# Gate and up products of a SwiGLU block: one 512-column product for the rounded weight against both activation halves, alternating with a 256-column product for the weight's low half

## What is computed

```
D_MODEL = 1024; SEQ = 256; DEPTH = 2; D_FF = 2816

def swiglu(x, wg, wu, wd):
    return (jax.nn.silu(x @ wg) * (x @ wu)) @ wd

for l in range(DEPTH):
    x = layer_norm(ALPHA * x + 0.5 * swiglu(x, ffn1_wg[l], ffn1_wu[l], ffn1_wd[l]), ln1_g[l], ln1_b[l])
    ...
    x = layer_norm(ALPHA * x + 0.5 * swiglu(x, ffn2_wg[l], ffn2_wu[l], ffn2_wd[l]), ln4_g[l], ln4_b[l])
```

## Time and profile before

| | us |
|---|---|
| three runs | 1675.73, 1677.74, 1677.77 |
| median | 1677.74 |
| the profiled execution | 1675.35 |
| its span, first to last instruction | 1673.5 |
| PE / PEld / DVE / ACT / POOL busy | 1616.8 / 1495.3 / 1109.6 / 757.1 / 291.8 |
| granted TensorE clock, mean | 0.993 |

### The profile page before, as it was taken

The page is one execution under the profiler, slowest core; times in us unless marked ns, Lnnn a source line. Parts: engine busy times, 40 slices in busy tenths (PEclk is TensorE's granted clock), DMA queues, the critical chain, the costliest instruction groups (busy, mean ns, idle before and its releaser), DMA issues.

```text
span 1673.5 us, 33031 instructions
## 1 busy us (share of the span) xinstructions
PE 1616.8 (97%) x14330; PEld 1495.3 (89%) x14330; DVE 1109.6 (66%) x1409; ACT 757.1 (45%) x977; POOL 291.8 (17%) x190
## 2 busy tenths in 40 slices
PE   8999999999999998999999999999999999999996
PEld 7899989989889987999889898899898989889995
DVE  4676599868456758444576756998674658574445
ACT  3554453652253544444455445346433535454442
POOL 1133420000000305101150434100000004040102
PEclk9999999999999999999999999999999999999998
DMA  7766644433446545666676566544334455456663
GB/s 200 223 183 176 201 139 141 128 121 107 125 114 193 174 137 146 186 187 185 203 184 183 175 181 184 152 142 130 96 116 128 131 197 166 141 157 181 187 188 115
DMA packets 380777, 267.84 MB, mean 160 GB/s; under 512 B 21117, under 2 KB 361561, under 8 KB 380633
## 3 DMA queue, kind: packets, MB, share of 16 engines
q1 hardware_dynamic: 377784, 255.25, 52.2%
q10 hardware_dynamic: 2848, 10.49, 1.7%
HBM read 264.66 MB, written 1.05 MB: 159 GB/s over the span
## 4 chain that ended last, share of the span: by engine, by line
PE 79%; DVE 15%; ACT 3%; issue 2%; DMA 1%; POOL 0%; SPq 0%; DVEq 0%; ACTq 0%; POOLq 0%
PE bank L714 15%; PE bank L715 14%; PE bank L716 14%; PE bank L727 7%; PE banks4to L716 6%; PE banks4to L715 6%; PE banks4to L714 6%; DVE ring_lo L1696 4%; PE bank L756 1%; DVE small L1715 1%; DVE x_tok L1710 1%; ACT ring_hi L1306 1%; PE banks4to L1096 1%; PE bank L1261 1%; PE bank L1245 1%
## 5 line engine op out<-in xcount | busy, mean ns | idle before, releaser
L1696 DVE TENSOR_TENSOR ring_lo<-ring_raw,ring_hi 128x1024 fp32r<-128x1024 f32 x438 | 585.3, 1342 | 373.2 <-ACT ring_hi L1306 369.9
L1306 ACT ACTIVATE ring_hi<-ring_raw 128x1024 fp32r<-128x1024 f32 x444 | 468.4, 1058 | 489.7 <-PE bank L716 276.3
L714 PE MATMUL bank<-xT_hi,ring_hi 128*128 128x256 f32 x2208 | 633.3, 287 | 9.3 <-DVE ring_lo L1696 8.9
L715 PE MATMUL bank<-xT_lo,ring_hi 128*128 128x256 f32 x2208 | 625.3, 283 | 0.0
L716 PE MATMUL bank<-xT_hi,ring_lo 128*128 128x256 f32 x2208 | 625.1, 283 | 0.0
L714 PEld LDWEIGHTS bank<-xT_hi,ring_hi 128*128 128x128 f32 x2208 | 423.9, 192 | 20.0 <-issue 10.4
L715 PEld LDWEIGHTS bank<-xT_lo,ring_hi 128*128 128x128 f32 x2208 | 424.0, 192 | 2.1 <-issue 0.5
L716 PEld LDWEIGHTS bank<-xT_hi,ring_lo 128*128 128x128 f32 x2208 | 423.9, 192 | 0.0
L2311 POOL TENSOR_TENSOR hT_lo<-work,hT_hi 128x512 fp32r<-128x512 f32 x44 | 78.8, 1792 | 509.8 <-ACT hT_hi L1306 509.5
L714 PE MATMUL banks4to<-ring_hi,hT_hi 128*128 128x512 f32 x352 | 138.1, 392 | 3.1 <-DVE ring_lo L1696 3.1
L716 PE MATMUL banks4to<-ring_hi,hT_lo 128*128 128x512 f32 x352 | 139.6, 397 | 0.0
(11 more groups left out here) (313 smaller groups left out, 2170.3 us busy)
## 6 DMA issues: line engine op xcount, KB each, us to landing
ring_raw<-in_w_in_dram SPq DMA_DIRECT2D x100, 512.0 KB, 3.9
ring_raw<-in_ffn_wg_dram SPq DMA_DIRECT2D x88, 512.0 KB, 3.8
ring_raw<-in_ffn_wu_dram SPq DMA_DIRECT2D x88, 512.0 KB, 3.8
ring_raw<-in_ffn_wd_dram SPq DMA_DIRECT2D x88, 512.0 KB, 3.6
ring_raw<-in_xa_wkv_dram SPq DMA_DIRECT2D x32, 512.0 KB, 3.9
ring_raw<-in_s_glu_w_dram SPq DMA_DIRECT2D x16, 512.0 KB, 3.4
ring_raw<-in_mix_w_out_dram SPq DMA_DIRECT2D x16, 512.0 KB, 3.6
ring_raw<-in_xa_wq_dram SPq DMA_DIRECT2D x16, 512.0 KB, 4.1
```

The costliest lines, as they stand in the source:

```text
L714: mm(o, a[0], b[0], start=first, stop=False, **kw)
L715: mm(o, a[0], b[1], start=False, stop=False, **kw)
L1306: return nc.scalar.activation(o, i, func, **kw)
L1696: st.mark(tt(lo_flat(n), raw_flat(n), hi_flat(i), ALU.subtract), s_lo["dve"])
```

## The change

1. `xT_hi` and `xT_lo` become one tensor `xT`, so that one access pattern (`xT_both[:, :, k, :]`) reads block k of hi and then of lo: two runs of 256, 2048 numbers apart.
2. Gate and up pieces outside `first_chunk`: per block of weights, one product of the rounded weight with both halves (512 columns, a whole bank), then one of the remainder with x hi (256 columns, into the first half of the bank). Two weight loads instead of three, and the same 768 columns.
3. A piece now fills a bank of its own (`BANKS_OF` 2 for g and u), and the two halves of the bank have to be added. DVE does it with four reductions over pairs per step (`add_halves`): the two gate pieces into `sil`, the two up pieces into `htmp`. silu then works in place in SBUF, and the multiply reads both operands from SBUF.
4. A bank is released by its own reduction (`ffn_halves_added`), not by the multiply. `lo_to` and `hi_to` calls are rearranged around that.

```diff
-BANKS_OF = {..., "g0": 1, "u0": 1, "g1": 1, "u1": 1, ...
+BANKS_OF = {..., "g0": 2, "u0": 2, "g1": 2, "u1": 2, ...
-        xTh_t, _ = sb("xT_hi", ND * T, F32R)
-        xTl_t, _ = sb("xT_lo", ND * T, F32R)
+        xT_t, _ = sb("xT", 2 * ND * T, F32R)
...
+        xT_both = view(xT_t, 0, 2, ND, T)
...
+        def sum_count(kind, j, m):
+
+            return 4 * (int(kind[1]) * (NF // 2) + j) + (2 if kind[0] == "u" else 0) + m + 1
...
-            if kind in ("g0", "u0"):
-                return s_h, j + 1
-            if kind in ("g1", "u1"):
-                return s_h, NF // 2 + j + 1
+            if kind in WIDE:
+                return s_sum, sum_count(kind, j, b)
...
+                elif kind in WIDE:
+                    o = claim(kind, j, m)
+                    both = o[:, :].rearrange("p (a t) -> p a t", a=2)
+                    hi, lo = take(kind, j, m)
+                    for k in range(ND):
+                        mm(both, hi[:, k, :], xT_both[:, :, k, :], start=(k == 0), stop=(k == ND - 1), skip_group_check=True)
+                        last = mm(o[:, 0:T], lo[:, k, :], src[0][:, k, :], start=False, stop=(k == ND - 1),
+                                  skip_group_check=True)
...
             def silu(i, j):
 
-                hi_to(f"u{i}", j, 0)
-                done_chunk(act, f"g{i}", j)
-                if layer[0] or i * (NF // 2) + j >= 2:
-                    act.wait_ge(*at(s_h, i * (NF // 2) + j - 1))
-                st.mark(f(sil[j % 2], banks[rota(f"g{i}", j)][:, :], ACT.Silu), s_silu)
+                hi_to(f"u{i}", j, 1, ahead=1, further=False)
+                act.wait_ge(*at(s_sum, sum_count(f"g{i}", j, 1)))
+                st.mark(f(sil[j % 2], sil[j % 2], ACT.Silu), s_silu)
...
             def hidden(i, j):
-                lo_to(f"u{i}", j, 1, 1)
-                dve.wait_ge(*at(s_silu, i * (NF // 2) + j + 1))
+                def add_halves(kind, m, o):
+                    dve.wait_ge(*at(s_piece, INDEX[(kind, j, m)] + 1))
+                    x = banks[rota(kind, j, m)]
+                    ins = v.tensor_reduce(o[:, m * T:(m + 1) * T], x.rearrange("p (a t) -> p t a", a=2), AX.X, ALU.add)
+                    if kind[0] == "g" or m == 0:
+                        return st.mark(ins, s_sum)
+                    st.then(ins, s_sum)
+
+                g, u = f"g{i}", f"u{i}"
+                lo_to(u, j, 1, further=False)
+                if layer[0] or i * (NF // 2) + j >= 2:
+                    dve.wait_ge(*at(s_h, i * (NF // 2) + j - 1))
+                add_halves(g, 0, sil[j % 2])
+                add_halves(g, 1, sil[j % 2])
+                lo_to(u, j, 1, 1, further=False)
                 if layer[0] or i * (NF // 2) + j >= 2:
                     dve.wait_ge(*at(s_hl, i * (NF // 2) + j - 1))
-                done_chunk(dve, f"u{i}", j)
-                st.mark(tt(htmp[j % 2], sil[j % 2], banks[rota(f"u{i}", j)][:, :], ALU.mult), s_h)
+                add_halves(u, 0, htmp[j % 2])
+                lo_to(u, j, 1, 2, further=False)
+                add_halves(u, 1, htmp[j % 2])
+                dve.wait_ge(*at(s_silu, i * (NF // 2) + j + 1))
+                st.mark(tt(htmp[j % 2], sil[j % 2], htmp[j % 2], ALU.mult), s_h)
```

20 lines of the change are left out of this document (12 added, 8 removed).

## The result

| | before | after |
|---|---|---|
| median of 7 runs each, same chip (lowest to highest) | 1676.20 us (1674.72 to 1677.83) | 1681.91 us (1681.22 to 1684.04) |
| ratio to before, 95% interval | | 1.0032 (1.0022 to 1.0042) |
| profiled execution, and its span | 1675.35, 1673.5 us | 1684.04, 1682.2 us |
| steady step of a SwiGLU block | 17.07 us | 16.85 us |

The changed kernel is slower: by 0.32% by the ratio of the runs, by 5.7 us between the two medians. What follows explains these 8.7 us.

The account below looks back on a forecast made before the run. PE was taken to bound steady steps, with DVE full in a few places. Terms -9.0 + 8.0 + 3.6 = +2.6 us gave 1678.0 profiled, a median of 1680.3 us; range 1665 to 1690, the forecast's own 1674 to 1687.

Parts of the forecast that it names:

- The gain on PE: Gate and up pieces where PE sets the pace: 1080 triples, each 0.0083 us shorter, -9.0 us in all.
- The walk through steps 5 to 7: First block of each layer: reductions in DVE's full queue make splits late for PE, 4.0 us a layer, +8.0 us.
- The changes of width: Rival, gate and up pieces: columns alone set the pace or 512 following 256 costs extra; no gain, 1689 us, chance 0.15.
- the silu's later start: ACT's silu waits for the second gate reduction, with rounding of the next down piece ahead of it; costs nothing.
- step 4's down split: First block: the split had some 0.9 us to spare and gets two reductions (1.3 us) ahead of it, 0.3 us late.
- The other blocks' starts: First two steps of the other three blocks: reductions delay splits beside POOL's work, 1.2 us each, +3.6 us.
- The reduction's mean: DVE's new reductions of 512 numbers out of PSUM: 0.69 us each, or 1.0 if the reductions are dear.
- the later `hT_lo` at the last block's end: At a block's end `htmp` comes 0.6 us later, which fits in the 1.87 us to spare; costs nothing.
- The rival with a pace of 0.216 us: Products of 512 columns run as plain F32 ones do: triple 0.336 us, gain 26 us, time 1663 us, chance 0.08.
- the comparison with 216 ns for 512 columns: The skill's formula gives 216 ns, the trace 232; the prediction said the trace meets it only in plain F32 products.
- The tests named: Signs to check: triple 0.352 us, steady step 16.8, reduction 0.69, step 6 with carry into 7 some 4 us longer.
- The bound on PE's waits: PE's waits for gate and up splits rise from 8.9 to 15 us or more; under 12, the price is wrong.

Follow-up runs that it names:

- a1_hoist: The changed kernel with ACT rounding the second down piece before it waits for silu's input, not behind silu; 1680.58 us, ratio 1.0020 to before.
- b3_adds_silu: The kernel before plus four reductions a step, with silu waiting for the second and ACT's roundings ordered as in the changed kernel; 1691.43 us, ratio 1.0081.
- a6_grouped: The changed kernel with a piece's eight products of 512 columns first and its eight of 256 behind them; 1676.33 us, ratio 0.9999 to before.
- a4_noadds: The changed kernel with each reduction replaced by a copy of one column, so the halves are not added; 1673.96 us, ratio 0.9981 to before.
- b2_adds: The kernel before plus four reductions of 512 numbers a step in DVE's queue, silu not waiting for them; 1689.92 us, ratio 1.0069.

## Why the prediction came out as it did, step by step

The forecast was no change to slightly slower, 1680.3, with the larger chance on slower; the time was 1681.9, within both ranges. That it came within 1.6 us is in part luck. The forecast added +2.6 to a median of three runs, 1677.7, which became 1676.2 with seven; between medians the change is +5.7, and between the profiled executions, in which the terms were reckoned, +8.7. Where the other executions differ from the profiled ones isn't on record. One thing that varies is the clock: in a1_hoist and in b3_adds_silu the same wait cost 1.0 to 1.4 us more in one layer than in the other. The terms:

**The gain on PE: -9.0 forecast, -7.5 measured (the -7.0 of the balance, and 0.2 in step 7 of each layer).** The mechanism holds, the steady step is 16.85 (16.8 forecast). The term was mis-sized in the pace: 1080 x 0.0069 = 7.5. I added a 0.232 from a row of products of one width to a 0.120 from another such row. Alternating, the pair takes 0.353. The changes of width, which I had as a rival (0.240 after the last product of 512 in the earlier trace rows), cost 4 to 5 ns a pair, as a6_grouped shows. 0.353 is also just where that rival was to decide.

**The walk through steps 5 to 7: +4.0 forecast for each layer, +7.0 measured (half of the 13.6 of the balance, and the 0.2 of gain).** This is the term that was mis-sized most. The first half of the walk was right in kind and place: both down splits were late. Set back by 0.52, by which PE is later at the first down piece already, the split of the second down piece began at 114.52 - 0.52 = 114.0 (forecast 112.8) and that of the next first one at 133.87 - 0.52 = 133.35 (forecast 132.1). Three things were missing:
- +1.2 us: the rounding behind the silu. The prediction said that the silu's later start costs nothing, with the rounding of the next down piece ahead of it. It is the first of the two that stands ahead; that of the second stands behind. I had followed it in a steady step, where DVE is free, and not in the crowded one. The waits of 6.86 and 1.04 us in the rows above show it, a4_noadds shows it without the reductions, and a1_hoist takes it away.
- +1.5 us or so: the clock. Neither the walk nor a rival had it. The two down pieces behind the 2.25 us wait took 7.2 us, from 135.23 to 142.43, where the kernel before took 5.6 for them. (The 4.21 us in step 6 cost nothing of their own, as far as the rows tell: PE waits for DVE again before step 7, 0.68 and then 2.25 us.)
- +0.4 us: step 4's down split, whose delay is seen in step 5, 0.7 instead of 0.3.

"In step 7 DVE has slack ... and the queue is caught up without more" was right for DVE, and wrong as a price: PE had already lost 6.6 us by the first gate piece of step 7, and nothing gives it back. b2_adds shows that the reductions alone are worth 6.7 a layer (some 5.5 with reductions as quick as those of the changed kernel), so that about half of the miss or more would have been there without the coupling. The parts don't add: in the table coupling alone makes 2.6, reductions alone 6.7, both 7.5, since they delay the same splits.

**The other blocks' starts: +3.6 forecast, +1.6 measured, and for another reason.** I let the reductions delay the second split by 1.6 to 1.9. b2_adds has the reductions there at no cost. The reason is in the ends of the splits:

```profile
663.20 2.81 DVE L1708 TENSOR_TENSOR ring_lo<-ring_raw,ring_hi 128x1024 fp32r<-128x1024 f32 x1
```

```profile
661.67 3.26 POOL L2325 TENSOR_TENSOR x_tok<-x_tok,work 128x1024 f32<-128x1024 f32 x1
665.01 3.25 POOL L2326 TENSOR_TENSOR x_tok<-x_tok,work 128x1024 f32<-128x1024 f32 x1
```

This split ends 1.08 us after POOL's operation does (666.01 and 664.93), and so does every split that began beside one, in both kernels. A split that begins a reduction later, but still beside POOL's operation, ends no later. The price of 3.1 us that I gave it was mostly a wait for POOL, and a reduction ahead of it fits into that wait. What costs is the multiply, which I held at 0.69 "with its operand in SBUF": 2.16 beside POOL. It is bound in the same way, ending 0.55 us after POOL's operation, and PE then waits 0.92 us for the split behind it. The warning of the Trainium skill, page "SBUF — State Buffer", section "Who interferes with whom", that `tensor_tensor` with both inputs in SBUF contends with GpSimd's reads and `tensor_reduce` doesn't, agrees with the rows on both: 2.16 and 2.70 for the multiply, 0.67 to 0.68 for reductions in the same stretch. I had quoted it and left it out of the sum.

**The rest.** The reduction's mean is 686 ns (0.69 forecast), the same as for operations that read 512 numbers without a stride. Two gate reductions ahead of a split, the release of the banks and the later `hT_lo` at the last block's end cost nothing in steady steps and at the end, as said. The +0.5 in step 2 of the very first block had no term. The rival with a pace of 0.216 us rested on a misreading: the products of the earlier trace rows have 256 columns, so their 0.216 says nothing of 512 columns, and the comparison with 216 ns for 512 columns has the same slip. In the runs 512 columns took 0.230 to 0.236.

**The tests named.** Triple and step came as forecast; step 6, with what it carries into 7, was to be some 4 us longer and was 6.3. The bound on PE's waits was badly chosen: those for gate and up splits went from 8.9 to 11.7 us (9.1 and 2.6 in the two rows), under the 12 that was to disprove the price, while the price was there and higher. The walk itself had put the lateness before down pieces; their row went from 3.1 to 11.6. I named the row that I had looked at before, not the one that the walk led to.
